# A blocked state-space recurrence becomes a rotated scan, in smaller pipelined batches, with its tables made in an earlier stage

## The reference, cut to what matters

```python
lam_bar = jnp.exp(lam[None] * dt[..., None])                 # complex, per direction, group, dimension
b_bar   = ((lam_bar - 1.0) / lam[None])[..., None] * b_mat
bu = jnp.einsum('dgph,btgh->dbtgp', b_bar, ug)               # inputs to the state
bu = jnp.stack([bu[0], jnp.flip(bu[1], axis=1)], axis=0)     # direction 1 runs backward
_, h = lax.associative_scan(combine, (a_el, bu), axis=2)     # h[t] = lam_bar * h[t-1] + bu[t]
h = h + decay_pow[:, None] * h0[:, :, None]                  # start state
y = jnp.real(jnp.einsum('dghp,dbtgp->dbtgh', c_mat, h))
y = (y[0] + jnp.flip(y[1], axis=1)) + d_skip * uf            # then gelu and a gate
```

## Time and profile before

| what | us |
|---|---|
| median of 3 runs (2881.11 to 2881.91) | 2881.35 |
| the profiled execution | 2880.15 |
| its span, first to last instruction | 2878.4 |
| PE / DVE / ACT / POOL busy in it | 2099.3 / 1307.0 / 719.6 / 648.2 |
| modulation, first DMA to the norm's first load (L228, at 109.82) | 109.1 |
| tables, first DMA (L476) to u's weight load (L353) | 52.0 |
| S5, first DVE instruction to GLU's weight load (L840) | 448.7 |

### The profile page before, as it was taken

One profiled execution on the slowest core, in us unless ns is written; L12 is line 12 of the kernel. 1 busy time (PEld: TensorE's weight loads), 2 busy tenths in 40 slices (PEclk: granted clock), 3 DMA queues, 4 the chain that ended last, 5 costly groups with the idle time before them and its releaser, 6 DMA issues. The chain is left out here.

```text
span 2878.4 us, 51105 instructions
## 1 busy us (share of the span) xinstructions
PE 2099.3 (73%) x21319; PEld 1367.3 (48%) x21372; DVE 1307.0 (45%) x2851; ACT 719.6 (25%) x1585; POOL 648.2 (23%) x726
## 2 busy tenths in 40 slices
PE   7514514034235569898998988994899999999998
PEld 1112313023223347776776777872455555555553
DVE  0253387886650244554645556433343332333235
ACT  0120101001031123443443434441233111221121
POOL 0121261230022012222222222221423121212144
PEclk9756667576577779899999999996999999999999
DMA  7510000000001000000000000003331110111012
GB/s 261 189 60 29 8 8 9 0 8 8 12 17 65 19 9 22 3 10 9 15 11 9 2 5 2 3 6 147 142 125 59 59 40 20 59 59 59 1 66 95
DMA packets 62643, 124.49 MB, mean 43 GB/s; under 512 B 4422, under 2 KB 24390, under 8 KB 61642
## 3 DMA queue, kind: packets, MB, share of 16 engines
q1 hardware_dynamic: 62428, 121.37, 12.4%
HBM read 106.63 MB, written 12.63 MB: 41 GB/s over the span
## 5 line engine op out<-in xcount | busy, mean ns | idle before, releaser
L82 PE MATMUL psum<-arena 128*128 128x384 bf16 (+3 forms) x2220 | 728.4, 334 | 130.2 <-POOL arena L922 29.0
L83 PE MATMUL psum<-arena 128*128 128x384 bf16 (+3 forms) x2234 | 734.4, 335 | 95.8 <-POOL arena L375 80.0
L84 PE MATMUL psum<-arena 128*128 128x384 bf16 (+3 forms) x2225 | 727.1, 333 | 0.5
L1455 ACT ACTIVATE arena<-psum 128x256 f32<-128x256 f32 (+5 forms) x900 | 291.8, 336 | 527.9 <-PE psum L1327 143.6
L82 PEld LDWEIGHTS psum<-arena 128*128 128x128 bf16 (+2 forms) x2244 | 222.9, 99 | 405.2 <-issue 82.3
L84 PEld LDWEIGHTS psum<-arena 128*128 128x128 bf16 (+2 forms) x2244 | 226.5, 101 | 171.0 <-issue 11.9
L83 PEld LDWEIGHTS psum<-arena 128*128 128x128 bf16 (+2 forms) x2244 | 224.4, 100 | 164.0 <-issue 8.6
L724 PE MATMUL psum<-arena 128*16 128x128 f32 (+1 forms) x128 | 29.1, 314 | 265.4 <-ACT arena L667 265.4
L2451 DVE TENSOR_TENSOR arena<-arena 128x384 f32<-128x384 f32 x96 | 101.8, 1060 | 239.3 <-ACT arena L2318 239.3
L1327 PE MATMUL psum<-arena 64*64 64x64 f32 x2880 | 181.4, 223 | 10.7 <-DVE arena L2004 10.7
L1326 PE MATMUL psum<-arena 64*64 64x64 f32 x2304 | 162.4, 230 | 8.1 <-DVE arena L2004 7.5
(11 more groups left out here) (294 smaller groups left out, 3258.1 us busy)
## 6 DMA issues: line engine op xcount, KB each, us to landing
arena<-in_w_ff SPq DMA_DIRECT2D x16, 2048.0 KB, 8.9
arena<-in_w_ada SPq DMA_DIRECT2D x12, 2048.0 KB, 7.9
arena<-in_x SPq DMA_DIRECT2D x18, 512.0 KB, 3.7
arena<-in_pos SPq DMA_DIRECT2D x18, 512.0 KB, 4.6
arena<-in_w_in SPq DMA_DIRECT2D x12, 512.0 KB, 4.1
x<-arena SPq DMA_DIRECT2D x9, 512.0 KB, 3.1
arena<-x SPq DMA_DIRECT2D x9, 512.0 KB, 3.3
out_y<-arena SPq DMA_DIRECT2D x9, 512.0 KB, 2.7
```

Of the source, the lines that this page charges most:

```text
L82: nc.tensor.matmul(out, whi, xhi, start=first, stop=False)
L83: nc.tensor.matmul(out, wlo, xhi, start=False, stop=False)
L84: return nc.tensor.matmul(out, whi, xlo, start=False, stop=last)
L1455: copy = lambda out, src: nc.scalar.activation(out, src, ACT.Copy)
```

## The change

In **modulation** the table work is a generator, `s5_tables`, on the same DVE: after each of the 12 bias adds (now written out, not looped) one piece of it runs. The eight small loads stand in SP's queue behind the first two weight loads. The stage of its own is gone; the tables live in memory taken before modulation. The tables differ: `turn` (16 rotations) and `lap` (8 coarse rotations) in place of the powers over spans, a real decay `rho` per chunk, and tap tables with both signs and two more taps (17 instead of 15).

In **S5** the complex recurrence is turned: the arrivals are multiplied by the conjugate of a rotation `rot` (made per batch from `lap` and `turn`), a real scan with the decay `rho` runs over all chunks of four groups in one instruction for each of the real and the imaginary part, and the states are rotated back. Batches are of 4 groups, 8 of them, all written out, most buffers double; each engine's order is shifted so that a batch's later steps stand beside the next one's first. The output weights `gout` are now a slice of POOL's f, copied by ACT; `strip` and the arrivals are copied out of PSUM by ACT.

```diff
-GB = 8
+SEG = NC_ + 1
+TAPS = 2 * CH + 1
+GB = 4
...
 def stage_modulation(nc, M, ins):
...
+            for v, n in ((s5_par, "ssm_par"), (s5_b[0], "ssm_b_re"), (s5_b[1], "ssm_b_im"), (S.c[0], "ssm_c_re"), (S.c[1], "ssm_c_im"),
+                         (S.h0[:, 0], "ssm_h_re"), (S.h0[:, 1], "ssm_h_im"), (S.d, "ssm_d")):
+                sp.dma_start(v, ins[n]).then_inc(ev("in"), 16)
...
-            with dve.Fori(0, 6) as i:
+            tables = s5_tables(nc, M, ev, dve, s5_par, s5_b)
+            for i in range(6):
                 for q in range(2):
                     dve.wait_ge(ev("products", q), i + 1)
...
                     nc.vector.tensor_tensor(mod[0:2, cols], ps[0:2, q, :], bada[0:2, cols],
                                             ALU.add).then_inc(ev("stored", q), 1)
+                    next(tables, None)
+            for _ in tables:
+                pass
             dve.wait_ge(ev("cols_t"), 1)
...
 def stage_s5(nc, M, ins, outs):
...
+        @block.gpsimd
+            for i in range(NBATCH):
+                need(pool, ev("tap"), 2 * (i - 1))
+                need(pool, ev("gout"), 2 * (i - 1))
...
+                mult(fr, c4[0], re)
+                mult(fi, c4[0], im_neg)
+                mult(tg[0], c4[1], im_neg)
+                mult(tg[1], c4[1], re_neg).then_inc(ev("f_products"), 1)
+                pool.wait_ge(ev("f_products"), i + 1)
+                nc.gpsimd.tensor_tensor(fr, fr, tg[0], ALU.add)
+                nc.gpsimd.tensor_tensor(fi, fi, tg[1], ALU.add).then_inc(ev("f"), 1)
...
+        @block.scalar
+            for i in range(NBATCH):
+                more = i + 1 < NBATCH
+                if more:
+                    weights(i + 1)
+                out_weights(i)
+                if more:
+                    taps(i + 1)
+                    decay(i + 1)
+                if i:
+                    context(i - 1)
+                if more:
+                    arrivals(i + 1)
+                natural(i)
...
+        @block.tensor
+            for i in range(NBATCH):
+                if i + 1 < NBATCH:
+                    arrive(i + 1)
+                    tap(i + 1)
+                if i + 2 < NBATCH:
+                    turn(i + 2)
+                outputs(i)
...
+        @block.vector
+            def spin(i):
+                full = [v.unsqueeze(1).broadcast_to([P, 2, GB, SEG]) for v in rot]
+                flat = lambda v: v.rearrange("p g s -> p (g s)")
+                dve.wait_ge(ev("arrived"), 4 * i + 4)
...
+                c.step(tt(X, V, full[0], ALU.mult))
+                c.step(tt(Y, V, full[1], ALU.mult))
+                c.settle(dve)
+                c.step(tt(V[:, 0], X[:, 0], Y[:, 1], ALU.add))
+                c.step(tt(V[:, 1], X[:, 1], Y[:, 0], ALU.subtract))
+                c.settle(dve)
+                dve.wait_ge(ev("rho"), 2 * i + 2)
+                for n in H2:
+                    c.step(nc.vector.tensor_tensor_scan(flat(V[:, n]), flat(rho[i % 2]), flat(V[:, n]), 0.0, ALU.mult, ALU.add))
+                c.settle(dve)
...
+            for i in range(NBATCH):
+                spin(i)
+                if i:
+                    latent(i - 1)
+                if i + 2 < NBATCH:
+                    in_weights(i + 2)
+                if i + 1 < NBATCH:
+                    rotor(i + 1)
+                    skip(i + 1)
+            latent(NBATCH - 1)
...
 def program(nc, ins, outs, scratch, upto=99):
...
-    stage_modulation(nc, M, ins)
...
     keep_front = A.at
-    stage_s5_tables(nc, M, ins)
+    s5_memory(M)
+    stage_modulation(nc, M, ins)
+    stage_norm(nc, M, "norm1", ins["x"], ins["pos"], 0, (M.hi, M.lo))
```

More of the change, by code:

```diff
@@ L448, in stage_s5_tables, with s5_tables @@
     S.in_table = two(CH, G)
[L449 to L453, removed]
+    S.tap_table = [A.take(TAPS, G) for _ in range(3)]
+    S.turn = two(SUP, G)
+    S.lap = two(LC // SUP, G)
+    S.rho = A.take(G)
     S.b = two(G, GC)
     S.c = two(G, GC)
-    S.h0 = two(G)
+    S.h0 = A.take(2, G)
     S.d = A.take(G, parts=GC)
     S.final = A.take(2, G)
-    keep = A.at
-    par = A.take(3, G)
-    b_raw = two(G, GC)
+def s5_tables(nc, M, ev, dve, par, b_raw):
+    A, S = M.arena, M.s5
+    two = lambda *s: (A.take(*s), A.take(*s))
     pw = two(CH + 1, G)
@@ L467, in stage_s5_tables @@
     t = (A.take(G * SUP), A.take(G * SUP))
[L468 to L575, removed]
@@ L576, in stage_s5_tables, with op, horner, whole @@
-    clear(nc, ev)
-    A.at = keep
+    c = Chain(ev("tables"))
+    ts, tt, stt = nc.vector.tensor_scalar, nc.vector.tensor_tensor, nc.vector.scalar_tensor_tensor
+    def op(ins_):
+        c.step(ins_)
+        c.settle(dve)
+    def horner(v, x, coefficients):
+        op(ts(v, x, coefficients[0], coefficients[1], ALU.mult, ALU.add))
+        for a in coefficients[2:]:
+            op(tt(v, v, x, ALU.mult))
+            op(ts(v, v, a, None, ALU.add))
+    def whole(v, x, scale):
+        op(ts(v, x, scale, 12582912.0, ALU.mult, ALU.add))
+        op(ts(v, v, 12582912.0, None, ALU.subtract))
@@ new lines, in s5_tables, with exponential @@
+    f32 = lambda x: float(np.float32(x))
+    def exponential(v, x):
+        whole(q0, x, 1.0 / math.log(2.0))
+        op(ts(q0, q0, -126.0, 127.0, ALU.max, ALU.min))
+        op(stt(out=q1, in0=q0, scalar=-0.693359375, in1=x, op0=ALU.mult, op1=ALU.add))
+        op(stt(out=q1, in0=q0, scalar=2.12194440e-4, in1=q1, op0=ALU.mult, op1=ALU.add))
+        horner(v, q1, [1 / math.factorial(n) for n in range(8, -1, -1)])
+        op(ts(q0, q0, 127.0, None, ALU.add))
+        op(ts(power, q0, 8388608.0, None, ALU.mult))
+        op(tt(v, v, power.bitcast(F32), ALU.mult))
@@ new lines, in s5_tables @@
+    dve.wait_ge(ev("in"), 8 * 16)
+    exponential(dt, ldt)
+    yield
+    op(tt(aim, lim, dt, ALU.mult))
+    op(tt(are, lam, dt, ALU.mult))
+    exponential(mag, are)
+    yield
+    whole(q0, aim, 1.0 / (2 * math.pi))
+    op(stt(out=red, in0=q0, scalar=-6.28125, in1=aim, op0=ALU.mult, op1=ALU.add))
+    op(stt(out=red, in0=q0, scalar=-f32(2 * math.pi - 6.28125), in1=red, op0=ALU.mult, op1=ALU.add))
+    op(stt(out=red, in0=q0, scalar=-f32(2 * math.pi - 6.28125 - f32(2 * math.pi - 6.28125)), in1=red, op0=ALU.mult, op1=ALU.add))
@@ new lines, in s5_tables @@
+    for _ in range(3):
+        twice()
+    yield
+    op(tt(mag, mag, mag, ALU.mult))
+    op(tt(mag, mag, mag, ALU.mult))
+    op(tt(S.rho, mag, mag, ALU.mult))
+    for tab in (S.turn, S.lap):
+        for n in range(2):
+            op(nc.vector.memset(tab[n][:, 0, :], 1.0 - n))
+    op(nc.vector.tensor_copy(S.turn[0][:, 1, :], cos))
+    op(nc.vector.tensor_copy(S.turn[1][:, 1, :], sin))
+    yield
+    for known, upto in ((1, 2), (2, 4), (4, 8), (8, SUP - 1)):
+        powers(S.turn, known, upto)
@@ L674, in _, with weights, decay @@
-            rounds(act, NBATCH, batch)
+            copy = lambda out, src: nc.scalar.activation(out, src, ACT.Copy)
+            def weights(i):
+                need(act, ev("v"), i - 1)
+                for b in H2:
+                    act.wait_ge(ev("turned"), 2 * i + b + 1)
+                    copy(wx[i % 2][:, 2 * b:2 * b + 2].rearrange("p g n l -> p (g n l)"), ps[:, TURNED[b], :]).then_inc(ev("wx"), 1)
+            def decay(i):
+                act.wait_ge(ev("zero"), 3)
+                need(act, ev("spun"), i - 1)
+                for part in (slice(1, LC), slice(LC + 1, SEG)):
+                    copy(rho[i % 2][:, :, part], S.rho[:, gs(i)].unsqueeze(2).broadcast_to([P, GB, part.stop - part.start]))\
+                        .then_inc(ev("rho"), 1)
@@ new lines, in context @@
+            def context(i):
+                act.wait_ge(ev("y"), 2 * i + 2)
+                if i > 1:
+                    act.wait_ge(ev("sent", i % 2), 16 * (i // 2))
+                copy(y_ctx[i % 2].rearrange("p t (g c) -> p g t c", g=GB),
+                     ps[0:CC, YCTX, :].rearrange("p (g t c) -> p g t c", g=GB, t=CH)).then_inc(ev("y_ctx"), 1)
+            weights(0)
+            decay(0)
+            arrivals(0)
+            taps(0)
+            for i in range(NBATCH):
[11 more added lines that the diff above has]
+                natural(i)
@@ L693, in batch, with tap @@
+            def tap(i):
+                pe.wait_ge(ev("f"), i + 1)
+                for b in H2:
+                    need(pe, ev("taps"), 2 * i + b)
                     for j in range(2):
                         g = 2 * b + j
[L695 to L698 removed]
@@ L728, in _, with outputs @@
-            rounds(pe, NBATCH, batch)
+                        for n in H2:
+                            last = mm(ps[0:GC, TAP, j * 256:j * 256 + (TAPS - 2) * GC], S.b[n][:, GB * i + g, :],
+                                      f[i % 2][:, n, g, 1:TAPS - 1].rearrange("p m c -> p (m c)"), start=(n == 0), stop=(n == 1))
+                    last.then_inc(ev("tap"), 1)
+            def outputs(i):
+                pe.wait_ge(ev("natural"), 3 * i + 3)
+                pe.wait_ge(ev("gout"), 2 * i + 2)
```

(20 more changed lines are left out.)

383 lines of the change are left out of this document (191 added, 192 removed).

## The result

The changed kernel takes **2673.53 us** (median of 4 runs, 2671.56 to 2673.86); the kernel before, on the same chip, 2881.63 (4 runs, 2881.11 to 2883.55). The ratio is 0.9277, with a 95% interval of 0.9265 to 0.9288. The forecast was 2672.0, in a range of 2645 to 2725.

What follows compares the result with a forecast made beforehand. Modulation was taken as PE-bound, the table stage as DVE alone, S5 as a DVE chain with one uncovered tail per batch. 2880.15 - 52.0 + 1.9 - 158.7 = 2671.3, plus 1.2 for the median: 2672 us, range 2645 to 2725.

Steps and rivals of the forecast that it cites:

- Table stage: Between norm and u: the stage where DVE alone makes the tables disappears, -52.0 us.
- Tables inside modulation: Modulation: table pieces hide beside PE's products; only the twelfth, for b_bar, runs uncovered behind the last add, +1.9 us.
- DVE's own work: S5: DVE's own instructions take 22.2 us per batch of four groups, 177.6 us for eight batches.
- POOL's share: S5: each of 48 POOL instructions takes 2.0 us from DVE, 96 us in all, bounds 83 to 110.
- the colliding rows: S5 before the change: DVE lost 18.4 us to ten POOL instructions, 1.84 each, scaled to 2.08 for the new size.
- rival B: S5: POOL's turns cost little, done where DVE waits for others; the 96 us fall away, 2576 us; chance 0.05.
- sign of over 3 us for the products of 1160: S5: if right, products of 1160 take 1.35 us alone and over 3 beside POOL.
- What lies beside: S5: PE, ACT and the toe DMAs fit beside DVE's 34 us period; waits costed at nothing, up to 3 us per batch.
- Rival C: S5: uncovered waits for PE's outputs return, at most 8 us in each of eight batches, 2736 us; chance 0.12.
- The tail: End of S5: from the last states to GLU's weight load, 16 us instead of 25.1.
- S5: Whole stage: 177.6 + 96 + 16 = 290 us, -159 us.

Runs made afterwards that it cites:

- x1: Changed kernel with POOL's six tap-factor operations of 1088 elements per batch moved to DVE, POOL idle in S5: 2633.1 us, ratio 0.9139.
- x2: Changed kernel with POOL's f made for the first two batches only, 36 POOL instructions of 1088 left out: 2596.05 us, ratio 0.9012.
- x4: Changed kernel with each engine's order unshifted, all parts of one batch before the next, same work: 2778.44 us, ratio 0.9645.
- x5: Changed kernel with the rotation table stored by group, so that rotor reads it without a stride: 2660.3 us, ratio 0.9236.
- x7: Changed kernel with POOL's six products and sums replaced by six memsets of the same size from the third batch on: 2602.08 us, ratio 0.9035.
- x3: Changed kernel with the tables and their loads in a stage of their own between norm and u: 2726.44 us, ratio 0.9467.
- x6: Changed kernel with x1 and x5 together, and the b_bar table piece joined to the one before it: 2623.15 us, ratio 0.9107.

## Why the prediction was right

**Table stage, -52.0.** Right: the norm's load to u's weight load shrank by 52.9; of that, 0.8 is norm 1, which takes 74.9 us instead of 75.75.

**Tables inside modulation, +1.9.** The mechanism is right, the size off: +3.2. The piece for b_bar runs behind the last add as forecast (106.69 to 110.74) and DVE's last instruction ends at 111.2 instead of 108.2. The forecast took the last add to stay where it was; it came 1.3 us later (106.08 against 104.79). Only one of the adds, at 75.36 behind the `turn` piece, had no idle time before it, so DVE held up one add at most, and little of the 1.3 us comes from there. The fifth add already came 0.9 us later (53.24 against 52.33), after 4.18 us of waiting for PE; PE had stood idle for its weights for 1.92 us before that product, against 1.24 in the kernel before. In x1, x2, x4, x5 and x7, whose modulation has the tables too, the last add comes at 105.04 to 106.29, in x3, without them, at 104.42. Why PE waits longer for its weights was not tried. The eight small loads did not take 0.4 us each to issue as in the earlier trace rows but up to 4.48, behind the weight loads; nothing waited for them.

**DVE's own work, 22.2 per batch.** Right: 21.6 in x1, less its tap factors (29.2 - 7.6); the 0.6 us too many are 5 us over eight batches. There `spin` takes 357.76 - 346.94 = 10.8 (forecast 11.0), `in_weights` 4.1 (4.2), `rotor` 375.97 - 370.06 = 5.9 (6.0). The scan, which the trace of before showed only with 128 elements, takes 2.63 / 2 = 1.3 for 580, as worked out from the earlier trace rows.

**POOL's share, 2.0 each.** Right: 2.04 by x2, 12.4 / 6 = 2.07 by one batch. The Trainium skill (SBUF — State Buffer, Who interferes with whom) says that the shared port is locked for the whole of the winner's instruction and that the loser waits until it is over. Priced by whole instructions, 2.30 each, the 48 would have taken 110 us; they took 48 x 2.04 = 98. The trace agrees with the lock, and the price from the colliding rows was the nearer one. The same section says that a POOL instruction that only writes does not hold a two-input DVE instruction; x7 agrees, with 1.35 us for the products beside memsets. Against rival B the prediction counted 8 of 9 instructions of `spin` with two SBUF inputs; it is all ten, as the scans are held too (4.59 us for two at 331.98, 2.63 alone). Its sign of over 3 us for the products of 1160 came in some batches only.

**What lies beside, nothing.** Right: DVE is busy 94% of S5, and most of its 18.4 idle us lie in the tail (7.36 before the last copy, 7.5 from its end to GLU's load), which leaves 3.5 us for eight batches. Rival C did not come.

**The tail, 16.** Right: the last state is written at 559.3, GLU's load is issued at 575.43.

**S5:** 8 x 21.6 + 98 + 16.1 = 287, measured 286.6, forecast 290.

**What the forecast did not have** is the last line of the table: the stages behind S5, unchanged, take 6.0 us longer. RWKV's opening stretch in the kernel before, and then the same work in the changed kernel, with a later stretch of each:
```profile
923.66:979.85 56.19, 33.62 (x180) 19.39 (x180) 6.27 (x21) 9.05 (x17) 8.83 (x9) 0.83 0.12 33
...
1970.69:2013.19 42.50, 17.58 (x60) 6.98 (x63) 6.95 (x4) 7.42 (x4) 12.21 (x4) 0.66 0.62 241
```
```profile
712.27:772.19 59.92, 38.72 (x180) 21.91 (x180) 6.26 (x21) 9.05 (x17) 8.86 (x9) 0.76 0.11 31
...
1763.18:1808.17 44.99, 19.34 (x63) 7.31 (x64) 6.95 (x4) 7.42 (x4) 12.22 (x4) 0.64 0.59 228
```
The first has the same 180 matmuls, 5.1 us longer, at a granted clock of 0.76 instead of 0.83 (both means between the levels of 1.2 and 2.4 GHz), and the stretch is 3.7 us longer; the second loses 2.5. DVE, ACT and POOL take what they took. All seven experiments have it too, 2.4 to 6.3 us. Why the clock is lower there was not tried and stays open. That the total came within 2 us of the forecast is luck: S5's 3.4 us too many and this 6.0 us too few nearly cancel, with modulation's 1.3 too few and the 1.3 too many of the two stretches before S5. The single terms are good to some 3 to 6 us, not to 2.

## What to carry to other kernels

Before work goes to POOL beside a DVE that has no idle time and reads two SBUF inputs, price it in DVE's time: here a POOL instruction of 1088 elements took 2.04 us from DVE, which does the same in 1.29. A stage whose engines wait for each other once per batch is first a matter of order: the shift by one batch brought 106 us, the scan with the smaller batches and the moved work 56. Work hidden behind another engine is covered one period at a time; a piece longer than that (7.2 us against 6.4) delays what follows it: in x6 0.9 us ahead of the last add, of the 1.4 saved behind it.

## What had not been expected of the hardware

The tiniest instructions pay as much for one of POOL's turns as longer ones: a copy of 68 elements went from 0.15 us to 2.1, a sum of 16x64 from 0.21 to 2.15, a sum of 580 from 0.76 to 2.93, some 2 us each. POOL's memsets left DVE's two-input products alone but held the copies from SBUF to SBUF (1.23 for two instead of 0.30). An issue of a small load on SP took up to 4.48 us right behind large weight loads, where it takes some 0.3 with the queue empty. And code that nobody changed took 0.3% longer (6.0 of 2090.7 us) at a lower granted clock, 0.76 against 0.83 in the stretch shown.
